# RWKV-7 scan of a three-block network: gate products whole at level five, state products in other PSUM banks, bonus sums on 64x64 blocks, VectorE's large operations spread

## The chip, the core and the metric

The kernel runs on one core of a Trainium2 chip. The metric is the device time of one execution in microseconds; smaller is better. Engines: TensorE (PE; PEld is its weight load), VectorE (DVE), ScalarE (ACT), GpSimd (POOL), SyncE (SP).

## The reference, cut to what matters

The whole kernel is a network over 512 positions of width 1024: an attention block, an RWKV-7 block, and a third block with two other recurrences, each with matrix products of some thousand columns. The change touches the RWKV-7 recurrence alone. It runs for 16 heads of 64 and in two directions `d` (forward and backward):

```python
def step(state, inp):                       # one position, one head
    r_t, w_t, k_t, v_t, kk_t, a_t = inp
    sa = einsum('bhvk,bhk->bhv', state, -kk_t)
    state = state * w_t + sa (x) (kk_t * a_t) + v_t (x) k_t
    return state, einsum('bhvk,bhk->bhv', state, r_t)
...
for d in range(2):
    decay = exp(-exp(-softplus(-(w0[d] + tanh(xw @ w1[d]) @ w2[d])) - 0.5))
    a = sigmoid(a0[d] + (xa @ a1[d]) @ a2[d])
    g = sigmoid(xg @ g1[d]) @ g2[d]                       # the gate product
    kd = k * (1 + (a - 1) * k_a)
    o = rwkv7_scan(r, decay, kd, v, kk, a)                # flipped for d == 1
    bonus = sum(r * kd * r_k, per head) * v               # the bonus sum
    dir_out.append((group_norm(o) + bonus) * g)
y = dir_out[0] + dir_out[1]
```

## The kernel before, in words

The scan is done in eight **pairs**: one pair is a tile of 128 rows, which holds two heads `e` of 64, by 512 positions. `over_pairs` (L394) unrolls `pair(parity, n, prev, nxt)` eight times on each engine. Features live in two sets, `F` for this pair and `G` (`feats[1 - parity]`), which holds the last pair's leftovers and then the next pair's features. All arithmetic here is fp32; the trace counts two matmul records for each fp32 product.

A pair has 512 positions in eight **chunks** of 64 (`CH`, `NCH`). It runs through three stages.

1. **Head.** TensorE computes the scores inside each chunk (`each_scored`, L880 and L883), then the variances of the last pair (L912). ScalarE copies the last pair's outputs (`o_sb`, L1494) and squares them (L1563), and then copies the scores `L` out of PSUM. VectorE starts the inverse with two `copy_predicated` (L2053) and two transposes (L2057). GpSimd masks `L` for the next level (`level_mask`, L2311).
2. **Levels 1 to 5.** A triangular inverse `T` is doubled in size five times. At each level and for both directions: TensorE `each` (L863), ScalarE copies half of it (`x_taken`, L1494 with 128x256), TensorE `each_half` (L902), VectorE adds it to `T` (L2066) and transposes (L2069). Beside it, TensorE does the two products with the LoRA weights for the next pair (`hidden_product`, L811), and at levels 3 and 4 the other products inside the chunks (`each_stacked`, L893). ScalarE takes the hidden products (L1426, L1429), the logarithms and inverse roots for the last pair's normalization (L1499, L1505) and the exponentials of the next pair's decays (`decays`, L1441, L1442, L1444). VectorE scans the decays for the next pair after level 1 (L1998, both directions), subtracts after level 2 (L2002), forms the bonus terms (L2076), masks the outputs after level 3 (L2082), and after level 4 finishes the last pair (L2025 to L2039) and forms `kd_factor` of the next (L2005). At the end of level 5 stands `each_turned` of the values (L871), which ScalarE takes (L1535).
3. **Chain.** Eight steps `j`, chunk after chunk, each waiting for the state of the one before. TensorE: state times `al` (L1004; L1001 at `j` = 0), ScalarE copies it (L1494 with 128x64), TensorE times `T` (L1019), VectorE and ScalarE each copy half of the result (L2096 and L1546), TensorE forms the state product (L1041) and the outputs (L1045, L1028, L1055), VectorE forms the new state (L2107 or L2110, "STT") and decays it for the step after (L2118, "the decay pair", one for each direction). In the gaps of the chain stand, on TensorE, two quarters per step: of the bonus sums in steps 0 to 3 (L922) and of the next pair's gate product in steps 4 to 7 (L930); on VectorE, `out_bonus` after steps 1 and 3 (L2019), `y_low` (L2044) at 4, and the next pair's features: L2009 at 3, L2011 at 4 and L2015 at 5, each for both directions.

GpSimd's own order in a pair is ten level masks, then `features` step 0 (L2295 and L2296 for each direction, when `kd_factor` is there), then `units` (L2307, after level 5), `features` step 1 (L2300 and L2303 for each direction), and the copy of the next values (L2288).

PSUM banks of direction `d`: `A`, `B`, `C`, `O` are banks 4d to 4d+3. `A` holds `each` and the chain's products, `B` the scores and `each_half`, then bonus sums and gate quarters; `C` the hidden products, the stacked products, then the state products; `O` the outputs. Semaphore names say what is ready; `n(per, c)` is the count that a pair waits for. Each engine executes in program order, and a wait holds everything behind it on that engine. Weights aren't loaded during the scan.

Of the kernel before, what the change touches and what calls it, by code (L numbers as in the profile page):

```python
# [16 lines left out]
P = 128  # L17
SEQ = 512
D = 1024
DT = D // P  # L20
# [195 lines left out]
def program(nc, t, out):  # L216

    ctx = ExitStack()
    with ctx:
# [357 lines left out]
        def _(pe):  # L577
# [337 lines left out]
            def pair(parity, n, prev, nxt):  # L915
                F = feats[parity]

                def bonus_quarter(x, q):
                    at = slice(q * P, (q + 1) * P)
                    if q == 0:  # L920
                        pe.wait_ge(sem("bonus_terms"), n(2, x + 1))
                    mm = nc.tensor.matmul(B[x][:, at], const("head_sum"), F[x]["kd"][:, at], start=True, stop=True)  # L922
                    if q == 3:
                        mm.then_inc(sem("bonus_ready"), 1)

                def gate_quarter(x, q):
                    at = slice(q * P, (q + 1) * P)
                    if q == 0:
                        pe.wait_ge(sem("bonus_done"), n(2, x + 1))
                    mm = nc.tensor.matmul(B[x][:, at], lora2[:, (4 + x) * P:(5 + x) * P], lo_g[x][:, at], start=True, stop=True)  # L930
                    if q == 3:
                        mm.then_inc(sem("z_ready"), 1)
# [16 lines left out]
                for l in range(1, LEVELS):  # L949
                    for d in range(2):  # L950
# [6 lines left out]
                        each(A[d], R[d]["LM"], R[d]["T"]).then_inc(sem("x_ready"), 1)  # L957
                    for d in range(2):
# [25 lines left out]
                        if l == 5 and d == 0:  # L984
                            pe.wait_ge(sem("v_staged"), n(1, 1))
                            pe.wait_ge(sem("turned"), n(4, 2))
                            each_turned(O[0], v_st, "center").then_inc(sem("scores_ready"), 1)
# [3 lines left out]
                for j in range(NCH):  # L991
# [15 lines left out]
                    if j:  # L1007
                        quarter(j, 0)
# [21 lines left out]
                    else:  # L1030
                        quarter(j, 0)
                    quarter(j, 1)
                    for d in range(2):
# [109 lines left out]
        def _(act):  # L1143
# [294 lines left out]
            def decays(n, F, d):  # L1438

                act.wait_ge(sem("decay_summed"), n(2, d + 1))  # L1440
                nc.scalar.activation(F[d]["ka"], F[d]["ro"], ACT.Exp, scale=DECAY).then_inc(sem("decays_ready"), 1)  # L1441
                nc.scalar.activation(F[d]["al"], F[d]["al"], ACT.Exp, scale=-DECAY).then_inc(sem("decays_ready"), 1)  # L1442
                act.wait_ge(sem("decays_ready"), n(6, 3 * d + 1))
# [67 lines left out]
            def pair(parity, n, prev, nxt):  # L1511
# [27 lines left out]
                for j in range(NCH):  # L1539
# [139 lines left out]
        def _(dve):  # L1679
# [311 lines left out]
            def features(n, F, ends_at, step):  # L1991

                for d in range(2):
                    r = F[d]
                    if step == 0:
                        dve.wait_ge(sem("z_taken"), n(6, 1 + d))
                        src, dst = (r["al"], r["ro"]) if d == 0 else (r["al"][:, ::-1], r["ro"][:, ::-1])
                        V_.tensor_tensor_scan(dst, const("carry", 0, SEQ), src, 0.0, ALU.mult, ALU.add  # L1998
                                              ).then_inc(sem("decay_scanned"), 1)
                    elif step == 1:  # L2000
# [462 lines left out]
```

## Time and profile before

| | |
|---|---|
| median of 3 runs | 2405.8 us (2405.16 to 2407.24) |
| profiled execution, its own time | 2402.95 us |
| its span, first to last instruction | 2400.8 us, granted clock 0.979 |
| PE busy | 2247.8 us (94%), 19640 matmuls |
| DVE, ACT, POOL busy | 1278.1, 944.7 and 853.5 us |
| the scan's pairs 1 to 7 | 901.6 to 1323.5 us of the span |
| pair 8 | 1323.5 to 1380.9 us |

Busy time of one engine is an average over stages with different limits. In the scan the instructions are short (0.1 to 4 us), and what counts is who waits for whom, which the timeline (start, duration, idle before and its releaser in brackets) and the chain of waits show.

### The profile page before, as it was taken

How to read it: one execution, taken by the hardware profiler on the slowest of the kernel's cores; microseconds unless marked ns; L12 is line 12 of the kernel's file. 1: busy time of each engine (PE TensorE's matmuls, PEld its weight loads, DVE VectorE, ACT ScalarE, POOL GpSimd, SP SyncE). 2: the span in 40 equal slices, each digit the busy share in tenths (PEclk: the TensorE clock that was granted, in tenths of full speed). 3: DMA queues.
4: the chain of work that ended last, by engine and by line, in shares of the span. 5: the costliest groups of instructions: out<-in, count | busy, mean ns of one | idle time of the engine just before them, and what ended most of it. 6: DMA issues, size and time to landing. Idle time of an engine off the chain costs nothing.

```text
span 2400.8 us, 46534 instructions
## 1 busy us (share of the span) xinstructions
PE 2247.8 (94%) x19640; PEld 1710.1 (71%) x19640; DVE 1278.1 (53%) x2035; ACT 944.7 (39%) x1681; POOL 853.5 (36%) x464
## 2 busy tenths in 40 slices
PE   8999989999979998888888889999998999999998
PEld 6885778888867547777777767777887666754476
DVE  5128254022165676777777625695213999736123
ACT  4238434233244434444444443564323222343133
POOL 2310334434413214444444333344431433430246
PEclk9999999999979999999999999999997999999999
DMA  4312222232212210000000122344222333222222
GB/s 144 118 53 78 67 73 89 87 106 88 88 42 85 91 42 8 9 6 10 10 10 10 38 70 79 100 177 136 88 95 73 113 114 114 88 88 79 70 92 83
DMA packets 49883, 180.71 MB, mean 75 GB/s; under 512 B 5600, under 2 KB 5856, under 8 KB 49440
## 3 DMA queue, kind: packets, MB, share of 16 engines
q1 hardware_dynamic: 46064, 166.89, 21.4%
q10 hardware_dynamic: 3632, 11.08, 1.2%
q8 instruction: 148, 2.42, 0.4%
q14 instruction: 39, 0.32, 0.0%
HBM read 167.39 MB, written 10.55 MB: 74 GB/s over the span
## 4 chain that ended last, share of the span: by engine, by line
PE 72%; issue 11%; DVE 8%; ACT 4%; POOL 4%; DMA 1%; POOLq 0%; ACTq 0%; DVEq 0%; SPq 0%
PE ps L601 15%; PE ps L602 15%; PE ps L603 15%; PE ps L604 6%; POOL ring_lo L2262 4%; PE ps L863 2%; PE ps L649 2%; PE ps L902 2%; PE ps L1098 1%; PE ps L893 1%; PE ps L720 1%; PE ps L735 1%; PE ps L710 1%; PE ps L1041 1%; PE ps L1119 1%
## 5 line engine op out<-in xcount | busy, mean ns | idle before, releaser
L2262 POOL TENSOR_TENSOR ring_lo<-ring,ring_hi 128x1024 fp32r<-128x1024 f32 x240 | 589.8, 2466 | 985.3 <-ACT ring_hi L1155 985.2
L603 PE MATMUL ps<-u_lo,ring_hi 128*128 128x512 f32 x968 | 384.5, 397 | 0.0
L1155 ACT ACTIVATE ring_hi<-ring 128x1024 fp32r<-128x1024 f32 x240 | 251.6, 1053 | 103.1 <-DMA ring<-in_wall 99.8
L601 PE MATMUL ps<-mlp_u_hi,ring_hi 128*128 128x512 f32 x512 | 204.8, 400 | 13.0 <-DVE u_lo L1741 8.7
L604 PE MATMUL ps<-arena,ring 128*128 128x512 f32 x480 | 210.5, 594 | 6.0 <-ACT arena L1624 3.3
L603 PEld LDWEIGHTS ps<-u_lo,ring_hi 128*128 128x128 f32 x968 | 183.7, 190 | 43.4
L601 PE MATMUL ps<-mid_hi,ring_hi 128*128 128x512 f32 x512 | 203.3, 397 | 2.6 <-POOL ring_lo L2262 2.6
L602 PE MATMUL ps<-mlp_u_hi,ring_lo 128*128 128x512 f32 x512 | 203.6, 398 | 0.0
L603 PE MATMUL ps<-mid_lo,ring_hi 128*128 128x512 f32 x512 | 202.5, 396 | 0.0
L602 PE MATMUL ps<-mid_hi,ring_lo 128*128 128x512 f32 x512 | 202.5, 395 | 0.0
L601 PE MATMUL ps<-in_u_hi,ring_hi 128*128 128x512 f32 x480 | 193.8, 404 | 5.8 <-POOL gs_lo L2362 2.8
L602 PE MATMUL ps<-in_u_hi,ring_lo 128*128 128x512 f32 x480 | 190.5, 397 | 0.0
L2311 POOL TENSOR_TENSOR ring<-ring,consts 128x512 f32<-128x512 f32 x80 | 117.7, 1491 | 188.4 <-ACT ring L1494 109.6
L604 PEld LDWEIGHTS ps<-arena,ring 128*128 128x128 f32 x480 | 90.2, 190 | 123.4 <-issue 109.6
L1906 DVE TENSOR_TENSOR arena<-ps,arena 128x512 f32<-128x512 f32 (+1 forms) x64 | 44.1, 691 | 236.1 <-ACT arena L1308 236.1
L601 PEld LDWEIGHTS ps<-mlp_u_hi,ring_hi 128*128 128x128 f32 x512 | 97.2, 190 | 38.7 <-DVE u_lo L1741 9.2
L601 PEld LDWEIGHTS ps<-in_u_hi,ring_hi 128*128 128x128 f32 x480 | 90.8, 189 | 42.7 <-issue 13.0
L601 PEld LDWEIGHTS ps<-mid_hi,ring_hi 128*128 128x128 f32 x512 | 96.2, 188 | 27.9 <-POOL ring_lo L2262 4.9
L602 PEld LDWEIGHTS ps<-mlp_u_hi,ring_lo 128*128 128x128 f32 x512 | 97.4, 190 | 22.8
L603 PEld LDWEIGHTS ps<-mid_lo,ring_hi 128*128 128x128 f32 x512 | 96.2, 188 | 23.3
L602 PEld LDWEIGHTS ps<-mid_hi,ring_lo 128*128 128x128 f32 x512 | 96.2, 188 | 22.9
L863 PE MATMUL ps<-arena,ring 64*64 64x64 f32 x2560 | 85.7, 219 | 26.6 <-DVE arena L2057 13.3
(435 smaller groups left out, 4456.5 us busy)
## 6 DMA issues: line engine op xcount, KB each, us to landing
ring<-in_wall SPq DMA_DIRECT2D x273, 512.0 KB, 3.6
s_tables<-arena ACTq DMA_DIRECT2D x16, 512.0 KB, 2.6
arena<-s_tables SPq DMA_DIRECT2D x16, 512.0 KB, 3.6
arena<-bias_lines SPq DMA_DIRECT2D x16, 448.0 KB, 4.3
arena<-in_lora SPq DMA_DIRECT2D x8, 384.0 KB, 3.1
h<-in_x SPq DMA_DIRECT2D x1, 2048.0 KB, 8.4
out<-arena ACTq DMA_DIRECT2D x8, 256.0 KB, 2.8
consts<-in_consts SPq DMA_DIRECT2D x1, 1216.0 KB, 14.5
```

What stands on the lines that cost most here:

```text
L601: nc.tensor.matmul(y, w_hi, high, start=x == 0, stop=False)
L602: nc.tensor.matmul(y, w_lo, high, start=False, stop=False)
L603: return nc.tensor.matmul(y, w_hi, low, start=False, stop=x == k - 1)
L604: return nc.tensor.matmul(y, ring[:, at:at + P], rhs(x), start=x == 0, stop=x == k - 1)
L649: mm = nc.tensor.matmul(bank(7)[:, b:b + 1], squares[:, b * P:(b + 1) * P], const("mean", 0, 1), start=first and b == 0, stop=last and b = ...
L710: nc.tensor.matmul(bank(score_bank(n), key_width(n)), qT[rows, at:at + P], kT[rows, keys + first * P:keys + end * P], start=True, stop=Tru ...
L863: mm = nc.tensor.matmul(out[rows, at], a[rows, at], b[rows, at], start=True, stop=True)
L902: mm = nc.tensor.matmul(columns_of_level(out[rows, at], l, h), a[rows, at], columns_of_level(b[rows, at], l, h), start=True, stop=True)
L1155: nc.scalar.activation(ring_hi[:, slot], ring[:, slot], ACT.Copy).then_inc(sem("weights_high"), 1)
L1906: TT(mid[:, at], out_bank(f"up{n}{part}", j), relu[j % 2], ALU.mult).then_inc(y_taken, 1)
L2262: G.tensor_tensor(ring_lo[:, slot], ring[:, slot], ring_hi[:, slot].bitcast(F32), ALU.subtract).then_inc(sem("weights_split"), 1)
L2311: G.tensor_tensor(chunks(R[d]["LM"]), chunks(R[d]["L"]), mask("level", d * LEVELS + l), ALU.mult).then_inc(sem("level_masked"), 1)
```

## The change

What it does:

- **Gate product.** The eight quarters in chain steps 4 to 7 are gone. In their place both directions' products are done whole (128x128 by 512 columns) at the end of level 5 of the pair before, in bank `C`. ScalarE takes them after chain steps 0 and 1 (before: after 5 and 7).
- **Bonus sums.** They stand in chain steps 2 to 5 (before: 0 to 3), go to bank `C`, and each quarter is two products of 64x64 by 128 columns in place of one of 128x128 by 128.
- **State products** go to bank `B` (before: `C`). `each_turned` of the values stands between the two `each` of level 5 (before: between the two `each_half`). The wait on `z_taken` ahead of the scores becomes one on the last pair's `bonus_done`.
- **Decays.** The subtraction (L2002) and the third exponential (L1442) are gone: `al` is formed from the shifted columns of `ro`, with a small extra operation for the first column of each chunk.
- **VectorE's order.** `copy_predicated` reads the scores from PSUM and is followed by its own transpose, one direction at a time. The scans stand after level 1 and after level 2, one each; bonus terms and masked outputs between the two directions of levels 3 and 4; the end of the last pair in pieces at levels 4 and 5. In the chain: `kd_factor` at steps 0 and 1, the sum of the last pair (`out_summed`) at 1, `decayed_kk` at 2 and 3, `out_bonus` at 3 and 5, `decayed_r` at 4 and 5, `y_low` at 6.
- **GpSimd's order.** `units` stands ahead of `features` step 0.

```diff
@@ TensorE @@
-                    mm = nc.tensor.matmul(B[x][:, at], const("head_sum"), F[x]["kd"][:, at], start=True, stop=True)
+                        if nxt:
+                            pe.wait_ge(sem("z_taken"), nxt(6, 5 + x))
+                    for e in range(2):
+                        rows = slice(e * HEAD, (e + 1) * HEAD)
+                        mm = nc.tensor.matmul(C[x][rows, at], const("head_sum")[rows, rows], F[x]["kd"][rows, at], start=True, stop=True)
...
-                    mm = nc.tensor.matmul(B[x][:, at], lora2[:, (4 + x) * P:(5 + x) * P], lo_g[x][:, at], start=True, stop=True)
...
-                    q = 2 * (j % 2) + half
-                    if j < 4:
-                        bonus_quarter(j // 2, q)
-                    elif nxt:
-                        gate_quarter(j // 2 - 2, q)
-                pe.wait_ge(sem("z_taken"), n(6, 6))
+                    if 2 <= j < 6:
+                        bonus_quarter(j // 2 - 1, 2 * (j % 2) + half)
+                if prev:
+                    pe.wait_ge(sem("bonus_done"), prev(2, 2))
...
+                        if l == 5 and d == 0:
+                            pe.wait_ge(sem("v_staged"), n(1, 1))
+                            pe.wait_ge(sem("turned"), n(4, 2))
+                            each_turned(O[0], v_st, "center").then_inc(sem("scores_ready"), 1)
...
+                    if nxt and l == 5:
+                        for d in range(2):
+                            pe.wait_ge(sem("turned"), n(4, 2 * d + 2))
+                            hidden_product(nxt, 2, d, 2)
...
-                                mm = nc.tensor.matmul(C[d][e * HEAD:(e + 1) * HEAD, 0:CH], F[d][("ka", "be")[e]][:, at],
+                                mm = nc.tensor.matmul(B[d][e * HEAD:(e + 1) * HEAD, 0:CH], F[d][("ka", "be")[e]][:, at],
@@ ScalarE @@
-                nc.scalar.activation(F[d]["al"], F[d]["al"], ACT.Exp, scale=-DECAY).then_inc(sem("decays_ready"), 1)
...
-                    if nxt and j in (5, 7):
+                    if nxt and j < 2:
                         if prev:
-                            act.wait_ge(sem("dir_gated"), prev(2, 2))
-                        feature(nxt, G, 2, j // 2 - 2, 1)
-                    if prev and j == 2:
+                            act.wait_ge(sem("dir_gated"), prev(2, j + 1))
+                        feature(nxt, G, 2, j, 2)
+                    if prev and j == 4:
                         y_high(prev)
@@ VectorE @@
+            def decayed_kk(n, F, ends_at, d):
+                r = F[d]
+                to, at, first = [(slice(1, CH), slice(0, CH - 1), 0), (slice(0, CH - 1), slice(1, CH), CH - 1)][d]
+                al, by = chunks(r["al"]), chunks(pair_tile(kk, n))
+                dve.wait_ge(sem("decays_ready"), n(4, 2 * (d + 1)))
+                V_.tensor_copy(ends_at[d], ends(r["ro"], d)).then_inc(sem("p_end_ready"), 1)
+                STT(out=al[:, :, to], in0=chunks(r["ro"])[:, :, at], scalar=-1.0, in1=by[:, :, to],
+                    op0=ALU.mult, op1=ALU.mult)
+                TS(al[:, :, first], by[:, :, first], -1.0, None, ALU.mult).then_inc(sem("al_ready"), 1)
...
-                                       chunks(R[d]["L"])).then_inc(sem("tt_started"), 1)
-                for d in range(2):
+                                       chunks(bank(4 * d + 1))).then_inc(sem("tt_started"), 1)
...
+                        if nxt and l <= 2 and d == 1:
+                            decay_sums(nxt, G, l - 1)
+                        if l == 3 and d == 0:
+                            bonus_terms(n, F, 0)
+                            bonus_terms(n, F, 1)
+                        if l == 3 and d == 1:
+                            masked_outputs(n, 0)
+                        if l == 4 and d == 0:
+                            masked_outputs(n, 1)
+                        if prev and l == 4:
+                            out_scaled(prev, d)
+                            out_with_bonus(prev, G, d)
+                        if prev and l == 4 and d == 1:
+                            out_gated(prev, G, 0)
+                        if prev and l == 5 and d == 0:
+                            out_gated(prev, G, 1)
...
-                    if j in (1, 3):
-                        out_bonus(n, F, j // 2)
-                    if prev and j == 4:
+                    if nxt and j < 2:
+                        kd_factor(nxt, G, j)
+                    if prev and j == 1:
+                        out_summed(prev)
+                    if j in (3, 5):
+                        out_bonus(n, F, j // 2 - 1)
+                    if nxt and j in (2, 3):
+                        decayed_kk(nxt, G, p_end[1 - parity], j - 2)
+                    if nxt and j in (4, 5):
+                        decayed_r(nxt, G, j - 4)
+                    if prev and j == 6:
                         y_low(prev)
-                    if nxt and 3 <= j < 6:
-                        features(nxt, G, p_end[1 - parity], j)
@@ GpSimd @@
-                    features(nxt, feats[1 - parity], 0)
                     for d in range(2):
                         pool.wait_ge(sem("dt_ready"), n(10, 9 + d))
                         units(d)
+                    features(nxt, feats[1 - parity], 0)
                     features(nxt, feats[1 - parity], 1)
```

## Rows read from the trace of the kernel before

**Rows 1.** Windows: span, busy PE, PEld, DVE, ACT, POOL (count), granted clock, DMA.

```profile
901.60:1323.50 421.90, 366.82 (x10216) 315.52 (x10216) 316.30 (x651) 197.33 (x509) 188.57 (x150) 1.00 0.03 9
1081.50:1120.50 39.00, 31.70 (x1068) 27.84 (x1068) 30.90 (x43) 21.78 (x39) 17.58 (x13) 1.00 0.05 14
1120.50:1143.70 23.20, 20.86 (x392) 17.13 (x392) 15.07 (x52) 7.16 (x36) 9.06 (x9) 1.00 0.01 3
1065.10:1069.30 4.20, 4.13 (x54) 3.49 (x54) 1.49 (x8) 0.87 (x4) 1.00 (x2) 0.59 0.02 4
```

**Rows 2.** Timeline, PE: chain start (L1001) and next scores (L880), pairs 1 and 7.

```profile
937.39 0.45 PE L1001 MATMUL ps<-sq,arena 64*64 64x64 f32 x8 [0.47 <-ACT sq L1535]
958.84 0.27 PE L880 MATMUL ps<-ring_hi_values 64*64 64x64 f32 x1 [0.30 <-ACT arena L1432]
1301.12 0.45 PE L1001 MATMUL ps<-sq,arena 64*64 64x64 f32 x8 [0.47 <-ACT sq L1535]
1323.55 0.27 PE L880 MATMUL ps<-ring_hi_values 64*64 64x64 f32 x1 [0.36 <-ACT arena L1432]
```

**Rows 3.** Chain of waits, head and levels of pair 4: start, us, what.

```profile
1093.48 4.33 DVE u L1998 x2
1104.67 1.05 issue
1112.26 1.43 issue
```

**Rows 4.** Timeline, levels of pair 4: start, us, engine, work, idle before.

```profile
1087.16 2.08 PE L863 MATMUL ps<-arena,ring 64*64 64x64 f32 x64 [1.61 <-DVE arena L2057]
1099.88 0.38 ACT L1494 ACTIVATE ring<-ps 128x256 f32<-128x256 f32 x1
1117.13 1.12 PE L902 MATMUL ps<-ring 64*64 64x32 f32 x32 [1.23 <-ACT ring L1494]
```

**Rows 5.** One line's instructions in pairs 2 to 7: whole 512-column products.

```profile
L912 PE MATMUL ps<-arena,consts x12: 592/645/697, 960.9 to 1265.7; 128*128 128x512 f32 x12
```

**Rows 6.** Timeline, POOL.

```profile
1084.07 3.45 POOL L2311 TENSOR_TENSOR ring<-ring,consts 128x512 f32<-128x512 f32 x2 [17.96 <-ACT ring L1494]
1088.39 2.50 POOL L2311 TENSOR_TENSOR ring<-ring,consts 128x512 f32<-128x512 f32 x2 [0.88 <-PE ps L863]
1125.33 1.27 POOL L2303 TENSOR_TENSOR u<-u 128x512 f32<-128x512 f32 x1
1126.56 1.27 POOL L2300 TENSOR_TENSOR ring_hi_values<-ring_hi_values 128x512 f32<-128x512 f32 x1
```

**Rows 7.** Timeline, DVE: before the scan and pair 1's head.

```profile
885.53 2.34 DVE L1998 TENSOR_TENSOR_SCAN u<-consts,u 128x512 f32<-128x512 f32 x2
896.26 3.44 DVE L2011 SCALAR_TENSOR_TENSOR u<-u,arena 128x512 f32<-128x512 f32 x2
903.46 0.73 DVE L2053 COPY_PREDICATED ring<-consts,ring 128x512 f32<-128x512 int32 x1 [1.07 <-ACT ring L1494]
```

**Rows 8.** Timeline, DVE: chains of pairs 3 and 4.

```profile
1125.84 2.03 DVE L2118 TENSOR_SCALAR arena<-arena 128x64 f32<-128x64 f32 x2
1129.60 0.41 DVE L2118 TENSOR_SCALAR arena<-arena 128x64 f32<-128x64 f32 x2
1135.87 1.29 DVE L2011 SCALAR_TENSOR_TENSOR u<-u,arena 128x512 f32<-128x512 f32 x2
```

**Rows 9.** Timeline, PE: chains of pairs 3, 4 and 8.

```profile
1065.17 0.41 PE L1041 MATMUL ps<-sq,u 128*64 128x64 f32 x4 [1.48 <-DVE sq L2096]
1128.78 0.34 PE L1041 MATMUL ps<-sq,ring_hi_values 128*64 128x64 f32 x4 [1.01 <-DVE sq L2096]
1379.04 0.28 PE L1004 MATMUL ps<-arena,ring_hi_values 64*64 64x64 f32 x4
1379.65 0.45 PE L1019 MATMUL ps<-arena 64*64 64x64 f32 x8 [0.21 <-ACT arena L1494]
1380.39 0.46 PE L1045 MATMUL ps<-arena,sq 128*64 128x64 f32 x8
```

More of the change, by code:

```diff
@@ L1006, in pair @@
                         mm.then_inc(sem("w_ready"), 1)
-                    if j:
-                        quarter(j, 0)
+                    quarter(j, 0)
                     for d in range(2):
@@ new lines, in decayed_r, with bonus_terms @@
+            def decayed_r(n, F, d):
+                dve.wait_ge(sem("p_end_ready"), n(2, d + 1))
+                dve.wait_ge(sem("al_ready"), n(2, d + 1))
+                TT(F[d]["ro"], F[d]["ro"], pair_tile(rT, n), ALU.mult).then_inc(sem("features_v"), 1)
+            def bonus_terms(n, F, d):
+                r = F[d]
+                dve.wait_ge(sem("features_p"), n(2, d + 1))
+                STT(out=r["kd"], in0=r["kd"], scalar=pair_col("r_k", n), in1=pair_tile(rT, n), op0=ALU.mult,
+                    op1=ALU.mult).then_inc(sem("bonus_terms"), 1)
@@ L2032, in out_gated, with out_scaled @@
-            def out_gated(n, F):
-                for d in range(2):
-                    dve.wait_ge(sem("with_bonus"), n(2, d + 1))
-                    STT(out=o_sb[d], in0=o_sb[d], scalar=pair_col("gn_b", n), in1=F[d]["g"], op0=ALU.add, op1=ALU.mult
-                        ).then_inc(sem("dir_gated"), 1)
+                TT(F[d]["kd"], pair_tile(vTr, n), bank(4 * d + 2), ALU.mult).then_inc(sem("bonus_done"), 1)
+            def out_scaled(n, d):
+                dve.wait_ge(sem("deviation_inverse"), n(2, d + 1))
+                TT(o_sb[d], o_sb[d], dev[d], ALU.mult).then_inc(sem("o_scaled"), 1)
@@ L2038, in out_gated, with out_summed @@
+            def out_summed(n):
                 dve.wait_ge(sem("dir_gated"), n(2, 2))
@@ L2119, in pair @@
                                ).then_inc(sem("state_decayed"), 1)
-                    if j in (1, 3):
-                        out_bonus(n, F, j // 2)
-                    if prev and j == 4:
+                    if nxt and j < 2:
[9 more added lines that the diff above has]
+                    if prev and j == 6:
                         y_low(prev)
-                    if nxt and 3 <= j < 6:
-                        features(nxt, G, p_end[1 - parity], j)
             first, last = (lambda per, c=0: c), (lambda per, c=0: (DT - 1) * per + c)
-            for step in range(6):
-                features(first, feats[0], p_end[0], step)
-            over_pairs(pair)
-            out_scaled(last, feats[(DT - 1) % 2])
-            out_gated(last, feats[(DT - 1) % 2])
+            for d in range(2):
+                decay_sums(first, feats[0], d)
+            for d in range(2):
+                kd_factor(first, feats[0], d)
+            for d in range(2):
+                decayed_kk(first, feats[0], p_end[0], d)
+            for d in range(2):
+                decayed_r(first, feats[0], d)
+            over_pairs(pair)
+            final = feats[(DT - 1) % 2]
+            for d in range(2):
+                out_scaled(last, d)
+            for d in range(2):
+                out_with_bonus(last, final, d)
+            for d in range(2):
+                out_gated(last, final, d)
+            out_summed(last)
             y_low(last)
```

98 lines of the change are left out of this document (27 added, 71 removed).

## The prediction

> **What bounds the kernel now.** I read the page first, then the windows, then the chain of waits and the timeline of whole pairs. PE is busy nearly everywhere, but in the scan it is full of records of 0.2 to 0.6 us that wait for other engines. Pairs 1 to 7 take 421.9 us [rows 1], 60.3 each; outside the scan nothing is changed. Pair 4 has 39.0 us of head and levels and 23.2 of chain. Over pairs 1 to 7 the chain, from its first product to the next pair's scores, takes 21.45 in the first and 22.43 in the last [rows 2]; the mean of the seven is 22.7.
>
> In the levels the end is set in turn by VectorE (4.33 us of two scans), by PE's own products, by gaps called "issue" (1.05 and 1.43 us in pair 4) [rows 3] and by ScalarE at level 5, where PE idles 1.23 us [rows 4]. "Issue" means that nothing recorded was awaited; I leave these gaps as they are.
>
> The chain is a loop PE, ScalarE, PE, VectorE, PE. With a fill of PE in both gaps a step takes 2.67 us (L1041 to L1041 where nothing is late). Without fills: L1004 to L1019 takes 0.61, L1019 to the product behind it 0.74 (both from pair 8's end) [rows 9], and L1041 to L1004 0.89 (pair 4), together 2.24.
>
> The rows that decide are those of VectorE beside GpSimd. Two scans take 2.34 us when GpSimd rests [rows 7] and 4.33 beside level masks [rows 3]; two masks take 2.50 alone and 3.45 beside `copy_predicated` [rows 6]. The decay pair takes 0.41 us alone and 2.03 in step 1 of pair 4 [rows 8]. That one starts at 1125.84 and ends at 1127.87; GpSimd's operations end at 1126.60 and 1127.83 [rows 6]. So each of the two waited for one whole GpSimd operation. Ahead of pair 1 two STTs with both inputs in SBUF take 3.44 us beside GpSimd [rows 7] and 1.29 alone [rows 8]. The engines alternate, one operation for one. A VectorE operation with an input in PSUM isn't held.
>
> The Trainium skill, "SBUF — State Buffer", section on the two separate sides, says that VectorE and GpSimd share a port pair as an exclusive lock, taken by VectorE in a two-port mode or with two SBUF inputs. The trace agrees with 2.03 against 0.41 us.
>
> **The change part by part.**
>
> Head. The scores no longer wait for the gate quarter's copy: 0.36 us [rows 2], which I count in the chain. `copy_predicated` now has its data in PSUM. Alone it took 0.73 us [rows 7]; beside masks two take 2.40 (from 1084.02 to 1086.42). The new form is in no row: bounds are 0.73 and 1.2 each, and I take 0.73, because PSUM inputs were never held. By the skill's rule (same page and section) a single SBUF input takes no lock, so the price would be 0.73 too; a copy still held would cost 0.5 us more per pair. With each transpose directly behind its copy, the first level's `each_half` comes about 1.1 us earlier against the start of the scores.
>
> Levels 1 and 2. One scan at a time: the 1.09 us that PE waited at level 3 go. Level 3 could start 2.2 us earlier. But ScalarE's queue (two sigmoids, table load, two logarithms, then the copy at 1099.88 [rows 4]) was ready only 0.1 us before PE needed it. It starts at the hidden product of level 2, which moves by 1.0 to 1.1. So 1.0 stays.
>
> Levels 3 and 4. The subtractions and the third exponentials (0.5 us each on ScalarE) were hidden behind PE. `masked_outputs(1)` moves behind the first update of level 4: about 1.2 us there, by which PE waits 0.5 before the last stacked products. 0.5 stays.
>
> Level 5. From the end of the stacked products to the chain took 6.56 us. Now PE does two `each` and the turned values (3.0), two `each_half` (2.1), then both gate products: four instructions of 128x512, like L912's four, 1.98 us (one is 0.6, and they overlap) [rows 5]. Sum 7.1, +0.5. ScalarE's work (copies 1.1, two exponentials 1.1, copy 0.4) fits below PE's 3.0. So nothing stays: 0 per pair, between -0.5 and +1.0, since denser PE work may lengthen or shorten the "issue" gaps.
>
> Chain on PE. Sixteen 128x128 products leave or shrink. Step 0 loses two fills, steps 1 and 6 both: 2.24 a step. Steps 2 to 5 keep bonus fills; the 64x64 form by 128 columns is in no row: between 0 and the old 0.42 us per quarter, step 2.24 to 2.67, taken 2.45. With step 0 the loop from the first product to the last is 1.1 + 2.24 + 2.24 + 4 x 2.45 + 2.24 + 0.8 = 18.4 us if nothing is late.
>
> Chain on VectorE beside GpSimd. This is where I differ from the intended effect. Before, GpSimd's first four feature operations ran at level 5 and step 0, the rest by step 2, and in the chain only decay pairs met them. Now `kd_factor` stands in steps 0 and 1, so all eight operations of 1.27 us [rows 6] and the copy run inside the chain, from about 3.2 us on. Count from the chain's first product:
> - Step 1: GpSimd works from 3.2 to 5.8. The decay pair is due at 4.45 and ends at 5.8; `kd_factor` 0.5 and `out_summed` 0.6 follow, and the next copies start at 6.95 instead of 5.6: 1.35 late.
> - Step 2: GpSimd's third and fourth operations end at 8.15 and 9.4. The decay pair is due at 8.1 and ends at 9.45. Then `decayed_kk(0)` has three operations (ends 0.1, STT 0.6, first columns 0.1) that read SBUF twice or in a two-port mode. Each can wait for one GpSimd operation; next copies at 12.6 to 13.9 against 9.3. I take 3.4 late.
> - Step 3: decay pair, `out_bonus` 0.6 (PSUM, not held), `decayed_kk(1)`: at least 0.6 late alone, 1.8 with two GpSimd operations left. I take 1.2.
> - Step 4: fits. Step 5: `out_bonus` and `decayed_r`: 0.3 late. Step 6: `y_low` has no decay pair beside it.
> Sum 6.3: the chain is 24.7 us against 22.7, +2.0 per pair (bounds: -2.9 if nothing is held, +3.2 if all is). Seven pairs: +14.
>
> Clock. After PE's stop of 1.48 us in pair 3 [rows 9] the granted clock of the next 4.2 us was 0.59 [rows 1], that is for the most part the lower level of 1.2 GHz; a step took 4.12 us instead of 2.67. After the stop of 1.01 us in pair 4 it stayed at full speed. A stop of 3 us in each chain should cost the same 1.4, partly under VectorE's lateness: 0.4 taken, +3 in all (0 to +10).
>
> Pair 8 has no next pair: no gate fills before or after, lighter steps 0, 1 and 6: -1.5. Before pair 1 GpSimd holds VectorE as before, with two more small operations, but the exponentials end earlier: 0, bounds -1 and +2. The end of the last pair keeps its order: 0.
>
> Sum: 0 + 14 + 3 - 1.5 = +15.5 us on a profiled time of 2402.95 (span 2400.8 and 2.15 around it): 2418.5. The median of the runs shown is 2.85 above the profiled one, so 2421.
>
> **Rivals.**
>
> A, faster: the spread works as meant. VectorE's small operations slip in between GpSimd's. For it: GpSimd waits for its own results between some operations, and a short VectorE operation can pass there. Against it: 2.03 us [rows 8] and the STTs ahead of pair 1. Then the lateness is 0.45 + 0 + 0.6 + 0.35 = 1.4, the chain 19.8, -2.9 per pair: 7 x -2.9 = -20, -1.5 for pair 8 and -2 in the levels: 2382.
>
> B, no change: `decayed_kk`'s small operations on 8 columns aren't held. Steps 2 and 3 lose about 2.5 us of lateness; the chain is 22.2 to 22.8 and the clock stays up. Total -3 to +2: 2405. It decides where GpSimd's remaining operations meet only one STT.
>
> C, slower still: all is held and the low clock lasts. 7 x (3.2 + 1.4) - 1.5 = +31: 2437. For it: pair 3's low clock after a shorter stop.
>
> D, PE's instruction supply is the bound in the levels: the gaps called "issue" grow by what the head and level 3 save. It costs up to 1 us per pair, +7 on any case; alone, with A, 2389.
>
> **How the numbers follow.** Held by GpSimd as summed: 0.47, 2421, its own range 2411 to 2431. C 0.13. A with or without D 0.24. B 0.16. A measurement of this kernel can tell 0.2% (4.8 us) from no change. Faster 0.27 (A and a part of B), same 0.12, slower 0.61. The range reaches to A's side with 2384 and to C's with 2437.
>
> **What would show it.** GpSimd's L2295 to L2303 all behind the chain's first product, and PE idle before L1041 in step 3 by 3 us with VectorE named: right. The decay pairs of steps 1 and 2 at 1.3 us or more. The two `copy_predicated` at 0.7 each beside masks of 1.25. Level 3's wait for L2066 gone, and one on ScalarE's copy in its place. Chain 24.7 us per pair, levels 38 as before. It is wrong if the decay pairs and `decayed_kk` run at 0.41 and 0.9 us while GpSimd works, or if the levels get shorter by more than 1 us per pair: then PE didn't pay for the gate products.

## The result, and the profile after

The median is 2415.95 us (17 runs, 2408.8 to 2420.9) against 2405.8; the ratio over all runs is 1.0038, with a 95% interval of 1.0027 to 1.0050. The change makes the kernel slower, by about 10 us. One run of the kernel before (3663.4 us) and one of the first experiment (4354.6 us) fell in a slower state and don't enter the ratios. The profiled execution took 2415.8 us, its span is 2414.0.

The windows of the changed kernel: pairs 1 to 7, then head and levels of pair 4, its chain, the middle of that chain, and pair 8 (columns as in [rows 1]).

```profile
901.69:1342.34 440.65, 365.92 (x10244) 306.07 (x10244) 314.55 (x651) 192.09 (x494) 192.09 (x151) 0.93 0.03 9
1089.51:1127.17 37.66, 33.02 (x1075) 28.04 (x1073) 25.58 (x38) 20.98 (x37) 15.63 (x12) 1.00 0.02 4
1127.17:1153.87 26.70, 19.91 (x394) 16.03 (x393) 20.14 (x56) 7.27 (x35) 11.39 (x9) 0.81 0.06 17
1134.47:1143.50 9.03, 5.85 (x112) 4.77 (x112) 8.11 (x17) 1.89 (x9) 8.07 (x7) 0.76 0.01 4
1342.34:1395.20 52.86, 44.92 (x1455) 39.66 (x1452) 36.19 (x82) 22.83 (x64) 17.30 (x12) 1.00 0.12 43
```

Pairs 1 to 7 take 440.65 us where they took 421.9 [rows 1]. The scan still begins at the same time (first scores at 901.69, before 901.63), and what comes behind it is 1.2 us shorter. In the table, head and levels of a pair run from its first scores to its chain's first product, and the chain from there to the next pair's scores, as in [rows 2]. The first two columns are means of pairs 1 to 7, in us; pair 8 is whole.

| | head and levels | chain | clock in the chains | pair 8 |
|---|---|---|---|---|
| before | 37.56 | 22.72 | 1.00, one at 0.93 | 57.30 |
| after | 36.80 | 26.15 | 0.81 to 0.87 | 52.86 |

So the chains lose 7 x 3.43 = 24.0 us, the levels give back 5.3, pair 8 4.4 and what is behind the scan 1.2: 13.1 of the span's 13.2.

Where the chain loses is plain on PE. These are its stops ahead of the state product (now L1036) in pair 4, for steps 2, 3 and 4 (counted from 0); the first line answers to [rows 9].

```profile
1134.47 0.34 PE L1036 MATMUL ps<-sq,ring_hi_values 128*64 128x64 f32 x4 [1.17 <-DVE sq L2105]
1139.92 0.48 PE L1036 MATMUL ps<-sq,ring_hi_values 128*64 128x64 f32 x4 [3.04 <-DVE sq L2105]
1144.40 0.48 PE L1036 MATMUL ps<-sq,ring_hi_values 128*64 128x64 f32 x4 [0.66 <-DVE sq L2105]
```

It waits for VectorE's copy of `u` (L2105). What VectorE did ahead of that copy, and what GpSimd did meanwhile:

```profile
1130.53 0.37 DVE L2105 COPY sq<-ps 64x64 f32<-64x64 f32 x2 [0.21 <-PE ps L1016]
1131.70 1.40 DVE L2127 TENSOR_SCALAR arena<-arena 128x64 f32<-128x64 f32 x2
1133.48 0.68 DVE L2054 TENSOR_TENSOR arena<-arena 128x512 f32<-128x512 f32 x1
1135.29 2.50 DVE L2127 TENSOR_SCALAR arena<-arena 128x64 f32<-128x64 f32 x2
1137.78 0.67 DVE L2006 SCALAR_TENSOR_TENSOR u<-u,arena 128x504 f32<-128x504 f32 x1
1138.38 1.23 DVE L2008 TENSOR_SCALAR u<-arena 128x8 f32<-128x8 f32 x1
1141.07 1.67 DVE L2127 TENSOR_SCALAR arena<-arena 128x64 f32<-128x64 f32 x2
1142.66 0.68 DVE L2031 TENSOR_TENSOR arena<-arena,ps 128x512 f32<-128x512 f32 x1
1143.93 0.16 DVE L2008 TENSOR_SCALAR u<-arena 128x8 f32<-128x8 f32 x1
1145.56 0.41 DVE L2127 TENSOR_SCALAR arena<-arena 128x64 f32<-128x64 f32 x2
```

```profile
1130.40 1.27 POOL L2322 TENSOR_TENSOR u<-u,arena 128x512 f32<-128x512 f32 x1 [4.31 <-DVE u L1996]
1133.64 1.65 POOL L2322 TENSOR_TENSOR ring_hi_values<-ring_hi_values,arena 128x512 f32<-128x512 f32 x1 [0.75 <-DVE ring_hi_values L1996]
1136.48 1.25 POOL L2327 TENSOR_TENSOR u<-u 128x512 f32<-128x512 f32 x1
1137.81 1.76 POOL L2330 TENSOR_TENSOR u<-u 128x512 f32<-128x512 f32 x1
1142.08 0.61 POOL L2315 COPY arena<-arena 128x512 f32<-128x512 f32 x1
```

All eight feature operations lie between 1130.4 and 1142.1, inside the chain (four of them are shown, and the copy behind them). While they run, the decay pair takes 1.40, 2.50 and 1.67 us, and 0.41 when they are over. The clearest line is the 128x8 operation: 1.23 us beside GpSimd, 0.16 when GpSimd is done. And the turn-taking goes both ways: the STT at 1137.78 takes its normal 0.67, the GpSimd operation begun at 1137.81 takes 1.76 instead of 1.25 (the STT was first, and had 0.64 of its time left), and the 128x8 operation behind ends at 1139.61, when that one is over. Operations with an input in PSUM are not held: the copies of `u` (L2105) take 0.37 at 1130.53, beside GpSimd, and 0.37 when it is done, and the masking of the head's second scores (L2074) takes 0.65 to 0.68 beside GpSimd's masks. No engine waits for a result of GpSimd in this chain, so it is not its data that VectorE or PE lack.

In the head, VectorE and then GpSimd, answering to [rows 6, 7]: the two copies from PSUM take 0.73 and 0.69 beside masks that stay at their undisturbed 2.5 for two. Level 3's wait is the third line.

```profile
1092.19 0.73 DVE L2068 COPY_PREDICATED ring<-consts,ps 128x512 f32<-128x512 int32 x1 [3.06 <-ACT ring L1488]
1093.59 0.69 DVE L2068 COPY_PREDICATED ring<-consts,ps 128x512 f32<-128x512 int32 x1
1107.76 1.06 PE L902 MATMUL ps<-ring 64*64 64x32 f32 x30 [1.35 <-ACT ring L1488]
1092.24 2.51 POOL L2338 TENSOR_TENSOR ring<-ring,consts 128x512 f32<-128x512 f32 x2 [13.81 <-ACT ring L1488]
```

### The profile page after: what moved, and what is told of

It reads as the page before. It is cut to its first block, busy times and chain, and to the rows that moved or that the text cites. A ratio compares the mean times of both kernels' runs of the same rounds, so it can differ in the third digit from the quotient of the medians.

```text
span 2414.0 us, 46629 instructions
## 1 busy us (share of the span) xinstructions
PE 2243.7 (93%) x19684; PEld 1698.9 (70%) x19684; DVE 1271.3 (53%) x2035; ACT 938.2 (39%) x1665; POOL 855.8 (35%) x464
## 4 chain that ended last, share of the span: by engine, by line
PE 72%; issue 11%; DVE 8%; POOL 4%; ACT 4%; DMA 0%; POOLq 0%; ACTq 0%; DVEq 0%; SPq 0%
PE ps L601 15%; PE ps L602 15%; PE ps L603 15%; PE ps L604 6%; POOL ring_lo L2289 4%; PE ps L902 3%; PE ps L863 2%; PE ps L649 2%; PE ps L893 1%; PE ps L811 1%; DVE arena L2127 1%; PE ps L1093 1%; PE ps L1036 1%; PE ps L720 1%; PE ps L735 1%
## 5 line engine op out<-in xcount | busy, mean ns | idle before, releaser
L601 PE MATMUL ps<-mlp_u_hi,ring_hi 128*128 128x512 f32 x512 | 204.5, 399 | 13.2 <-DVE u_lo L1735 8.9
L602 PEld LDWEIGHTS ps<-in_u_hi,ring_lo 128*128 128x128 f32 x480 | 91.4, 190 | 21.2 <-issue 0.2
```

The lines of the kernel that those rows point to most:

```text
L601: nc.tensor.matmul(y, w_hi, high, start=x == 0, stop=False)
L602: nc.tensor.matmul(y, w_lo, high, start=False, stop=False)
```

## The experiments

Theory 1: GpSimd's feature operations, now inside the chain, hold VectorE's small operations, PE waits, and its clock falls. The rivals are given with each run. Chain, levels and steps are read as in the table above; a ratio is to the kernel before on the same chip.

**GpSimd's feature operations on 8 columns.** The products that form the features are left out for the other 504 columns (and two ScalarE functions are changed so that the values stay bounded).

```diff
-    G.tensor_tensor(r["kd"], r["kd"], pair_tile(kTr, n), ALU.mult).then_inc(sem("kd_ready"), 1)
+    G.tensor_tensor(*cut(n, r["kd"], r["kd"], pair_tile(kTr, n)), ALU.mult).then_inc(sem("kd_ready"), 1)
... (`cut` takes [:, 0:8] of each tile; the other three operations likewise)
```

> The changed kernel with GpSimd's eight feature operations of each pair cut from 512 to 8 columns (and be and ka filled with small values, so that numbers stay finite): most of the feature products are left out. VectorE's instructions, their order and every wait stay. Theory 1, GpSimd's operations hold VectorE's in the chain: the stops of TensorE before the state products of steps 2 and 3 (1.17 and 3.04 us) fall below 0.7, the decay pairs of steps 1 to 3 run at 0.41 us, the chain takes 19.8 to 20.5 us in place of 26.15, the time is about 2375 us. Theory 2, VectorE simply has too much to do in these steps: the stops stay, the chain stays above 24, the time within 10 us of the changed kernel's.

2369.0 us (median of three runs), ratio 0.9855 (0.9826 to 0.9885). Chain 19.51 us, levels 36.58, clock 1.00; time and chain came somewhat lower than theory 1 said. Its windows (pairs 1 to 7, chain of pair 4), and VectorE in steps 2 and 3 of that chain:

```profile
900.30:1292.95 392.65, 346.63 (x10245) 289.63 (x10245) 278.02 (x650) 188.57 (x494) 127.48 (x150) 1.00 0.03 10
1103.90:1123.46 19.56, 16.59 (x393) 13.21 (x393) 14.89 (x56) 6.90 (x35) 2.38 (x9) 1.00 0.08 23
```

```profile
1108.42 0.41 DVE L2127 TENSOR_SCALAR arena<-arena 128x64 f32<-128x64 f32 x2
1112.33 0.16 DVE L2008 TENSOR_SCALAR u<-arena 128x8 f32<-128x8 f32 x1
```

VectorE has the same instructions in the same order, and the whole loss of the chain is gone, and more. Theory 1 holds; VectorE's own work and its new order are not the cause by themselves.

**PE kept busy.** The state products of steps 2 and 3 are preceded by 1 and 3 products of 128x128 by 384 whose result nobody reads, so that PE's stops get shorter while VectorE is as late as before.

```diff
+                    if half == 1 and nxt:
+                        for _ in range({2: 1, 3: 3}.get(j, 0)):
+                            nc.tensor.matmul(B[0][:, P:SEQ], const("head_sum"), const("carry", 0, SEQ)[:, P:SEQ], start=True, stop=True)
```

> The changed kernel with useless products added on TensorE in the chain, ahead of the state products of steps 2 (one of 128x128 by 384 columns) and 3 (three of them), where TensorE waits anyway; nothing is left out. Theory 1, the stop of 3.04 us takes the granted clock down and the low clock costs two steps: the clock stays at 1.00 in the chain, steps 4 and 5 take 2.4 to 2.7 us in place of 3.7 to 4.2, the chain 23.5 to 24 in place of 26.15, the time is about 2400 us. Theory 2, the clock falls for another reason or costs nothing, since these steps wait for VectorE: time 2416 us or a little more.

2411.5 us, ratio 1.0027 (1.0013 to 1.0040). The stop of 3.04 us is 0.91, and every chain of pairs 1 to 7 has the clock at 1.00, though one step later, where no filler stands, PE stops for 1.54 us:

```profile
1121.04:1145.48 24.44, 19.57 (x401) 14.57 (x400) 19.75 (x56) 6.89 (x35) 11.41 (x9) 1.00 0.06 19
```

```profile
1133.80 0.34 PE L1039 MATMUL ps<-sq,ring_hi_values 128*64 128x64 f32 x4 [0.91 <-DVE sq L2108]
1137.75 0.34 PE L1039 MATMUL ps<-sq,ring_hi_values 128*64 128x64 f32 x4 [1.54 <-DVE sq L2108]
```

The chain is 24.38 against 26.15: the low clock costs 1.77 us per pair. In pair 4 the steps, from one state product to the next, are 2.24, 3.59, 5.45, 3.95, 2.34 and 2.74 us against 2.24, 2.58, 2.61, 2.93, 2.34 and 2.74 with GpSimd's operations cut short: holding costs 1.01 + 2.84 + 1.02 = 4.87, and the means of the seven chains give the same (24.38 - 19.51). The median is only 4.5 us lower, 2411.5 where some 2400 was expected, and the two intervals overlap: in the time the filler's gain isn't clear of noise. The profile is that of the fastest of ten runs (2405.97 us, granted clock 0.978); the slowest took 2417.05 at 0.972. In the profile pair 8, which has no filler, ran its chain at 0.89 and took 55.98 us against 52.86; so the low clock moved there in part. Where the others lost their time no profile shows.

**`kd_factor` at the end of level 4**, so that GpSimd can begin earlier; its features of step 0 again stand ahead of `units`.

```diff
+                        if nxt and l == 4 and d == 1:
+                            if prev:
+                                dve.wait_ge(sem("with_bonus"), prev(2, 2))
+                            kd_factor(nxt, G, 0)
+                            kd_factor(nxt, G, 1)
...
-                    if nxt and j < 2:
-                        kd_factor(nxt, G, j)
@@ GpSimd @@
+                    features(nxt, feats[1 - parity], 0)
                     for d in range(2):
...
-                    features(nxt, feats[1 - parity], 0)
```

> The changed kernel with kd_factor of both directions behind the first out_gated at level 4 on VectorE, and GpSimd's features step 0 ahead of units, as before the change; nothing is left out. Theory 1, the place of GpSimd's operations sets the lateness: they begin some 5 us before the chain and end in step 2, the stop before the state product of step 3 falls from 3.04 to under 1.2 us, the chain takes 21 to 23 us in place of 26.15, the levels stay within 0.5, the time is about 2390 us. Rival: VectorE's order in the chain is the cause, or the two kd_factor lengthen level 5: less than 1 us per pair is won, 2409 or more.

2384.0 us, ratio 0.9915 (0.9892 to 0.9939): where two operations of 0.54 us stand, and with them GpSimd's, decides the sign of the change. Chain 20.67, levels 36.99; both the time and the chain are better than theory 1 said. The chain of pair 4:

```profile
1110.93:1131.61 20.68, 16.61 (x393) 13.20 (x392) 16.24 (x54) 6.89 (x35) 8.62 (x9) 1.00 0.07 22
```

**The kernel before, with its `kd_factor` moved into chain steps 0 and 1** and `units` ahead of the features: that one part of the change alone. (`features` step 2 is `kd_factor` of both directions; it gets a direction to pick.)

```diff
-                        if nxt:
-                            features(nxt, G, p_end[1 - parity], 2)
...
+                    if nxt and j < 2:
+                        features(nxt, G, p_end[1 - parity], 2, j)
@@ GpSimd @@
-                    features(nxt, feats[1 - parity], 0)
                     for d in range(2):
...
+                    features(nxt, feats[1 - parity], 0)
```

> The kernel before with one part of the change alone: kd_factor in chain steps 0 and 1 (one direction each) in place of the end of level 4, and GpSimd's units ahead of its features; nothing is left out, the other features of VectorE stay at steps 3 to 5. Theory 1, GpSimd's operations in the chain are enough to make it late: the decay pairs of steps 1 to 3 wait, the chain takes 23.5 to 24.5 us in place of 22.7 and the time is 2410 to 2417 us. Rival, they harm only together with decayed_kk at steps 2 and 3: the chain stays within 0.4 of 22.7, time within 3 us of the kernel before.

2415.7 us, ratio 1.0040 (1.0026 to 1.0054): alone it makes a loss as large as the whole change's, though not of the same parts (below). Windows of pairs 1 to 7 and of the chain of pair 4, and the longest stop in it:

```profile
902.56:1339.35 436.79, 372.23 (x10217) 319.18 (x10217) 327.58 (x651) 197.06 (x509) 189.77 (x150) 0.98 0.03 9
1129.90:1154.29 24.39, 20.99 (x392) 17.10 (x393) 17.73 (x53) 7.17 (x36) 10.76 (x10) 1.00 0.01 3
```

```profile
1144.72 0.34 PE L1041 MATMUL ps<-sq,ring_hi_values 128*64 128x64 f32 x4 [1.22 <-DVE sq L2096]
```

The chain is 24.32 us, about what the changed kernel has with the filler, 1.6 more than in the kernel before: 11.2 us in seven pairs. In this profile pair 1's levels add 5.0 us (40.76 against 35.76), since the clock fell twice there, and the other levels, pair 8 and what lies around the scan give back 4.6. Here PE has its old fills and `decayed_kk` isn't in step 2, the longest stop is 1.22, and the clock stays at 1.00 in the chains of pairs 1 to 7. So the way from 22.72 to 26.15 has two parts: +1.6 from GpSimd's place, and +1.8 from all the rest of the change. The filler's run gives 1.77 for the low clock; that the fewer fills and the longer wait behind `decayed_kk` cancel otherwise is what these sums leave, not a thing measured by itself.

**The gate product on 8 columns** at level 5, the gate left out.

```diff
-                            hidden_product(nxt, 2, d, 2)
+                            nc.tensor.matmul(C[d][:, 0:8], lora2[:, (4 + d) * P:(5 + d) * P], lo_g[d][:, 0:8],
+                                             start=True, stop=True).then_inc(sem("z_ready"), 1)
```

> The changed kernel with the gate products at the end of level 5 cut from 512 to 8 columns: the gate is left out. Theory 1, these 2 us lie on the path between level 5 and the chain: levels shorter by 1.7 to 2.0 us per pair for pairs 1 to 7, time about 2403 us. Rival, they are hidden behind ScalarE's copies and VectorE's last update of the inverse: under 0.7 us per pair, 2411 or more.

2408.3 us, ratio 1.0016 (1.0004 to 1.0027), where theory 1 said 2403. Levels and chain of pair 4:

```profile
1086.55:1121.31 34.76, 31.82 (x1076) 27.95 (x1073) 25.45 (x38) 20.98 (x37) 15.34 (x12) 1.00 0.02 4
1121.31:1147.80 26.49, 21.18 (x394) 17.26 (x393) 18.94 (x57) 7.65 (x35) 11.69 (x10) 0.74 0.06 17
```

The levels are 34.86, 1.94 less per pair, the four products' 1.98 us [rows 5] nearly one for one; but the chains are 0.3 longer at a clock of 0.74 to 0.87, and pair 8, in which the edit changes nothing, is 1.35 longer. PE does pay in full for the gate products at level 5. In five of the seven chains the clock now falls twice, the first time within 2 us of the chain's start. In pair 4 that is at 1122.19, when PE had made no stop above 0.33 us in the 8 us before; its first step takes 3.33 us in place of 2.25. So the gate products, too, were work that held the clock.

**The head as before**: `copy_predicated` from SBUF, both copies ahead of both transposes.

```diff
-                                       chunks(bank(4 * d + 1))).then_inc(sem("tt_started"), 1)
+                                       chunks(R[d]["L"])).then_inc(sem("tt_started"), 1)
+                for d in range(2):
```

> The changed kernel with the head's VectorE work as before the change: copy_predicated reads the scores from SBUF, and both copies stand ahead of both transposes; nothing is left out. Theory 1, what the head wins goes through to the chain: levels longer by 1.0 to 1.3 us in every pair, time about 2425 us. Rival, ScalarE's queue at level 3 sets the end of the levels whatever the head does: levels longer by less than 0.4, time 2416 us.

2429.5 us, ratio 1.0095 (1.0068 to 1.0123). Two copies take 2.41 us again, the levels 38.24, 1.44 more per pair (1.2 in pairs 2 to 7). This run also shows the price of the clock within one kernel, since one of its chains kept it (pairs 5 and 6):

```profile
1195.69:1222.39 26.70, 20.02 (x394) 16.13 (x393) 20.14 (x56) 7.28 (x35) 11.40 (x9) 0.81 0.06 17
1261.37:1285.94 24.57, 17.00 (x394) 13.41 (x393) 19.86 (x56) 7.18 (x36) 11.40 (x9) 1.00 0.07 18
```

**Both scans after level 1**, as before.

```diff
-                        if nxt and l <= 2 and d == 1:
-                            decay_sums(nxt, G, l - 1)
+                        if nxt and l == 1 and d == 1:
+                            decay_sums(nxt, G, 0)
+                            decay_sums(nxt, G, 1)
```

> The changed kernel with both scans after level 1, as before the change; nothing is left out. Theory 1, ScalarE's queue (sigmoids, table load, logarithms, then its copy for level 3) is later than VectorE's scans: TensorE waits at the start of level 3 instead of at its each_half, and the levels change by less than 0.3 us per pair, time 2416 us. Rival, spreading the scans was worth the 1.1 us that TensorE waited for them before: levels longer by 0.8 to 1.2, time about 2423 us.

2420.9 us, ratio 1.0057 (1.0032 to 1.0083), between both theories; levels 37.56, 0.76 more than with the scans apart, and 0.4 more without pair 1. This decides nothing; it is repeated below on a base with less scatter.

**The spread of VectorE's work later**: `kd_factor` at level 4 as above, `out_summed` at step 2, `decayed_kk` at 3 and 4, `decayed_r` at 5 and 6, when GpSimd is done.

```diff
-                    if prev and j == 1:
+                    if prev and j == 2:
                         out_summed(prev)
...
-                    if nxt and j in (2, 3):
-                        decayed_kk(nxt, G, p_end[1 - parity], j - 2)
-                    if nxt and j in (4, 5):
-                        decayed_r(nxt, G, j - 4)
+                    if nxt and j in (3, 4):
+                        decayed_kk(nxt, G, p_end[1 - parity], j - 3)
+                    if nxt and j in (5, 6):
+                        decayed_r(nxt, G, j - 5)
```

> As the run with kd_factor back at level 4 (2384 us), and VectorE's operations that read SBUF twice moved behind GpSimd's in the chain: out_summed at step 2, decayed_kk at 3 and 4, decayed_r at 5 and 6; nothing is left out. Theory 1, they no longer meet: steps 1 to 3 take 2.3 to 2.7 us, the chain 19.3 to 19.9 in place of 20.7, time about 2377 us. Rival, what remains is VectorE's own load, which only moves to the later steps: chain within 0.4 of 20.7, time 2382 to 2386.

2378.9 us, ratio 0.9885 (0.9859 to 0.9912); again on another chip:

> The same kernel as e9_spread_later, run again as the base of the next two, since its chains keep the full clock and small terms in the levels can be read with less scatter. Theory 1: ratio 0.988 to 0.990, chain 20.0 to 20.2 us per pair, levels 36.9 in pairs 2 to 7. A rival, that the first timing was a lucky one: above 0.991.

2375.9 us, ratio 0.9881 (0.9864 to 0.9898). Chains 20.07 and 20.19, levels of pairs 2 to 7 36.93 and 36.79. It beats both kernels. Against the run with `kd_factor` alone (20.67 us of chain, 2384.0) the chains are 0.5 to 0.6 shorter, between what theory 1 and the rival said, and the intervals of the two times overlap. The chain of pair 4 in the first of the two runs, with the decay pairs of steps 0 and 1, which are still held, and PE's wait behind:

```profile
1109.98:1130.10 20.12, 16.60 (x393) 13.16 (x392) 16.27 (x54) 6.88 (x35) 8.19 (x9) 1.00 0.08 23
```

```profile
1112.27 1.64 DVE L2132 TENSOR_SCALAR arena<-arena 128x64 f32<-128x64 f32 x2
1115.04 1.44 DVE L2132 TENSOR_SCALAR arena<-arena 128x64 f32<-128x64 f32 x2
1116.79 0.34 PE L1036 MATMUL ps<-sq,ring_hi_values 128*64 128x64 f32 x4 [0.16 <-DVE sq L2110]
```

The first held pair still costs about 0.5 us (the step behind it takes 2.76 against 2.24), the second nothing (2.57 against 2.58): little, when nothing long stands behind it in its step.

**On that version, both scans after level 1** (the edit is that of the run on the scans above).

> e9_spread_later with both scans after level 1, as in the kernel before. Theory 1 (ScalarE's copy for level 3 is ready just before PE needs it, so splitting the scans gives nothing): levels within 0.3 us per pair of e9b_spread_again and the time within 2 us of it. Rival (splitting the scans is worth the wait that PE had at level 3): levels +0.8 to +1.2 in pairs 1 to 7 with PE waiting for VectorE's first turn of level 3, time 5 to 8 us above e9b.

2382.5 us, ratio 0.9907 (0.9890 to 0.9923), 6.6 us above its base on the same chip, no run below the base's highest there. That is the time that the rival said. But pairs 2, 3, 4, 6 and 7 have levels of 37.00 us against 36.96. PE in level 3 of pair 4, first of this kernel (waiting for VectorE's scans), then of its base (waiting for ScalarE):

```profile
1088.96 2.20 PE L863 MATMUL ps<-arena,ring 64*64 64x64 f32 x64 [1.09 <-DVE arena L2080]
```

```profile
1088.35 1.06 PE L902 MATMUL ps<-ring 64*64 64x32 f32 x30 [1.35 <-ACT ring L1488]
```

In these pairs one wait takes the place of the other, as theory 1 has it. The difference of the profiles' levels is in pair 5 (38.94 against 35.96), where the scans' wait was followed by an "issue" gap of 1.61 us and the clock fell, and in pair 1 (38.02 against 36.79). So each theory has half: the levels of five pairs are theory 1's, the time is the rival's. That the median's 6.6 us come from such falls fits these two windows, but it isn't shown: it rests on one profile each. The windows are of this kernel, pair 5, around and behind the gap:

```profile
1149.00:1153.00 4.00, 2.38 (x104) 2.27 (x103) 2.43 (x4) 3.12 (x5) 0.64 (x1) 0.90 0.03 6
1153.00:1157.00 4.00, 4.00 (x134) 4.00 (x132) 2.31 (x4) 0.38 (x1) 0.61 (x1) 0.68 0.03 8
```

**On that version, `copy_predicated` from SBUF with its new order kept.**

```diff
-                                       chunks(bank(4 * d + 1))).then_inc(sem("tt_started"), 1)
+                                       chunks(R[d]["L"])).then_inc(sem("tt_started"), 1)
```

> e9_spread_later with copy_predicated reading the scores' copy in SBUF, but its order kept (each copy followed by its own transpose). It tells the source from the order, which e5_head_undo undid together. Theory 1 (the two-port form waits for one mask of GpSimd, about 1.2 against 0.7 us each, and both stand on the path): levels +0.5 to +1.1 per pair, time 4 to 9 us above e9b. Rival (the order alone made the gain, since the second copy's wait lies beside the first direction's work): levels within 0.3, time within 2 us.

2382.4 us, ratio 0.9908 (0.9893 to 0.9924), 6.5 us above the base, as theory 1 said. In pairs 2 to 7 the levels are only 0.34 longer, near the rival; pair 1's are 5.0 longer. There the copies take 1.03 and 1.01 instead of 0.73 and 0.69, PE stops for 2.09 us instead of 1.63. The clock falls during this stop in both kernels; in the base it is back by 910, here it stays low until 917.5 (windows of this kernel, then the base):

```profile
904.66 3.68 PE L863 MATMUL ps<-arena,ring 64*64 64x64 f32 x64 [2.09 <-POOL ring L2341]
```

```profile
910.00:920.00 10.00, 10.00 (x158) 7.70 (x159) 4.51 (x7) 2.66 (x6) 2.80 (x2) 0.62 0.01 2
```

```profile
910.00:920.00 10.00, 10.00 (x342) 9.20 (x340) 8.42 (x11) 5.70 (x10) 6.35 (x4) 1.00 0.01 3
```

So of the head's gain in pairs 2 to 7 the smaller part is the source; the order (each copy followed by its transpose) would give the rest, about 1.2 - 0.3 = 0.9 us per pair. That is an estimate from two different bases, and the levels of single pairs differ by up to 1.7 us within this profile.

## Why the prediction was right

Forecast 2421 us, measured 2415.95; slower was the likeliest sign, and the mechanism is the forecast one: all GpSimd's feature operations behind the chain's first product, the decay pairs of steps 1 and 2 at 1.40 and 2.50 us, and a stop of 3.04 before the state product of step 3. By its steps, in us per pair, with the measured value from the runs above:

- **Chain without GpSimd and at full clock**: forecast 18.4 and VectorE's own lateness 1.4 (the terms of rival A, together 19.8); measured 19.51.
- **VectorE's whole lateness**: forecast 6.3 on the 18.4; measured 24.38 - 18.4 = 6.0. Of this GpSimd's part is 1.01 in step 1, 2.84 in step 2 and 1.02 in step 3, 4.87 in all; the rest, 1.1, is VectorE's own. Step 2 was forecast 3.4 with a range of 3.3 to 4.6; of `decayed_kk(0)`'s three operations only the last was held (1.23), not the STT, which began right behind the held decay pair and 0.03 us ahead of GpSimd's next operation. Step 5 was forecast 0.3 late: PE stops 0.41 us behind it in pair 4, and the step takes 2.74 us with or without GpSimd.
- **Clock**: forecast 0.4 (0 to 1.4) a pair, measured 1.77, above its own range. This is the most mis-sized term. I took most of the low clock to lie under VectorE's lateness. In pair 4 the clock falls at 1139.09, while PE stops, and is back at 1149.33. In between PE works from step 3 on, where VectorE holds it up no longer or by 0.66 us, at the lower level: 4.48, 3.76 and 3.08 us a step against 3.95, 2.34 and 2.74. With the change's bare steps but no long stop (the first run) the clock stays at 1.00 in these chains, so the missing fills alone don't lower it; with a filler in the stops it stays too. The kernel before with `kd_factor` in the chain keeps 1.00 as well, but its longest stop is 1.22 us: what a 3-us stop would do among the old fills no run shows. Nor is a long stop the only way: without the gate products the clock also falls at the chain's start.
- **Chain in all**: forecast 24.7 + 0.4, measured 26.15. Seven pairs: +24.0 against +17.
- **Head and levels**: forecast 0 (-3.5 to +7 in all), measured -0.76 a pair, -5.3, below its range too. The copies from PSUM at 0.7 and masks at 1.25 each came as forecast, and so did level 3, where ScalarE's copy took over VectorE's wait (1.35 where I had 1.0). Level 5's stretch of 6.56 became 6.71, not 7.1: the gate products cost their full 1.94 as the run without them shows, but waits for ScalarE of 1.23 and 0.47 [rows 2, 4] went. From level 3's stacked products (1100.41 and 1107.76) to level 5 (1113.82 and 1120.19) pair 4 got 0.98 shorter, 0.47 of it in "issue" gaps. I had given all the levels' gains away and kept one.
- **Pair 8**: forecast -1.5, all of it in the chain, measured -4.4: 3.15 in head and levels, which I had left out (it gets the head's gain and pays for no gate product), and 1.3 in the chain, whose clock is 1.00 where the profile of the kernel before has 0.93.
- **Rival D**: PE's "issue" gaps in pairs 1 to 7 were 13.6 us in all and are 13.5. They did not grow.
- **Profile and median**: I added 2.85 us, by which the median before lay above its profiled run. After, it lies only 0.15 above: 2.7 of the 5 us between forecast and result are this term and no mechanism.

The errors partly cancelled: the clock term was 9.4 us too small (12.4 against 3), levels and pair 8 together 8.2 too large, the held chain 2.4 too large and the part behind the scan, taken as 0, 1.2. The near hit of the total is luck in part, better than the sum deserved; the sign is not luck, since it rests on [rows 6 to 8].

The Trainium skill, "SBUF — State Buffer", section on the two separate sides, says of the shared pair that "the other fully blocks" for the whole instruction. The 1.23 us of a 0.16-us operation in the trace agree, as does the 1.76 of GpSimd.

## What to carry to other kernels

When work is moved within a loop, follow what it releases on the other engines: `kd_factor` takes 0.5 us for a direction, but it gates 11 us of GpSimd work, and where that work falls was worth about 30 us here (ratios 1.0038 and 0.9915). Beside GpSimd, price every VectorE operation that has both inputs in SBUF, or copies or scales from SBUF to SBUF, by GpSimd's operation and not by its own size, count how often the turn changes, and put such operations where GpSimd rests. Work in a gap of TensorE that seems to cost nothing can be what holds its clock (1.77 us per chain here): before taking it out, ask which stops will then stand alone.

## What was not expected of the hardware

- A VectorE operation of 8 columns (0.16 us) took 1.23 us beside GpSimd. Splitting small work off doesn't make it cheap there.
- The price of a stop on TensorE is paid later. With stops of 1.17 and 3.04 us within 6 us the chain's mean clock was 0.81, between the levels of 1.2 and 2.4 GHz, and the cost was 1.8 us per chain. With one of 2.09 at pair 1's start the window from 910 to 920 ran at 0.62. A stop of 1.22 in a chain with fills, and one of 1.54 in the chain with the filler, left it at 1.00.
- No long stop is needed: with the gate products cut short the clock fell 0.9 us into pair 4's chain, behind stops of at most 0.33 us.
- A filler that holds the clock in one place didn't give its whole gain: 12.7 us less in the profile's pairs 1 to 7, 4.5 in the median, and that not clear of noise.
